# A decoder layer on one core: state products, rotation table and weight rounding in the front stage, last two token tiles in one round

## The reference

```
mod = silu(c) @ w_ada + b_ada                     # 6 vectors: sh1 sc1 g1 sh2 sc2 g2
u = modulate(rmsnorm(x), sh1, sc1) @ w_in          # 1024 columns
pool_out = pooling windows 2/4/8/16 of u[:, :512], minus u, then a 128x128 matrix per group
ssm_out  = state space mixer of u[:, 512:], 32 groups of 16 columns, 64 complex states each:
           h[t] = lambda * h[t-1] + B u[t];  y = Re(C h) + D u;  gelu(y) * sigmoid(gelu(y) @ glu_w + glu_b)
x = x + g1 * (concat(pool_out, ssm_out) @ w_out)
h2 = modulate(rmsnorm(x), sh2, sc2)
router: softmax over 4 groups, top 1; top 2 of its 4 experts; gated MLP experts (hidden 256)
x = x + g2 * moe(h2);  y = rmsnorm(x)
```

## Time and profile before

| what | us |
|---|---|
| median of 3 runs | 1243.48 (1240.98 to 1244.09) |
| profiled execution | 1243.06, its span 1241.1 |
| busy: PE, PEld, DVE, ACT, POOL | 1049.5, 798.2, 755.6, 514.4, 258.4 |
| 262 to 324, last block of the front: PE, DVE | 54.07, 9.60 of 62 |
| 324 to 336, PE and DVE | 0.00 and 0.17 of 12 |
| 392 to 469, scans and outputs y: PE, DVE | 70.92, 67.32 of 77 |
| 469 to 680, token tiles: PE, DVE | 201.16, 141.53 of 211 |
| 722 to 1150, experts: PE | 401.41 of 428 |
| DVE, front: first four w_lo parts; powers after them | 54.32 + 4.63; 58.86 to 64.42 |
| ACT, modulating one turned k-step (L667) | 0.778, median |
| DVE beside POOL, 128x256 two-input passes from 227.06 on | 227.06 + 0.41, then 227.39 + 1.28 and the next at 228.71 |
| POOL, busy stretches from 283 on | 282.86 to 284.35, 288.29 to 296.33, 302.08 to 303.35 |
| DVE, tile 15: residual ends, mean starts, h2 done | 692.92, 694.15, 697.31 |
| DVE, sample tile 16: the same | 701.20, 702.41, 705.55 |
| last logits | 710.21 + 0.17 |

### The profile page before, as it was taken

The page is one execution under the profiler, slowest core; times in us unless marked ns, Lnnn a source line. Parts: engine busy times, 40 slices in busy tenths (PEclk is TensorE's granted clock), DMA queues, the critical chain, the costliest instruction groups (busy, mean ns, idle before and its releaser), DMA issues. The chain is left out here.

```text
span 1241.1 us, 18046 instructions
## 1 busy us (share of the span) xinstructions
PE 1049.5 (85%) x5428; PEld 798.2 (64%) x5429; DVE 755.6 (61%) x1234; ACT 514.4 (41%) x764; POOL 258.4 (21%) x319
## 2 busy tenths in 40 slices
PE   5599999997568999997999535999999999999910
PEld 3266676674446767786888424887778878778710
DVE  2746475750289983367887686555676555555336
ACT  2522333221152235444665313455655544445325
POOL 0025252534131000000000001233333332232210
PEclk9699999998779999998999857999999999999955
DMA  9814646474592549466766457698789878765479
GB/s 304 324 35 115 205 114 201 118 228 162 147 198 90 167 140 265 157 175 233 239 209 224 134 201 250 163 293 217 218 263 267 223 212 222 220 154 110 88 206 394
DMA packets 173443, 244.74 MB, mean 197 GB/s; under 512 B 70519, under 2 KB 130631, under 8 KB 170263
## 3 DMA queue, kind: packets, MB, share of 16 engines
q1 hardware_dynamic: 148617, 180.31, 45.6%
q0 software_dynamic: 12528, 45.62, 16.1%
q10 hardware_dynamic: 12246, 18.14, 4.2%
HBM read 167.79 MB, written 75.84 MB: 196 GB/s over the span
## 5 line engine op out<-in xcount | busy, mean ns | idle before, releaser
L120 PE MATMUL experts_psGU<-weights_we_hi,experts_x_hi 128*128 (+1 forms) x344 | 144.9, 421 | 8.2 <-DVE experts_x_lo L2344 6.5
L121 PE MATMUL experts_psGU<-weights_we_hi,experts_x_lo 128*128 (+1 forms) x344 | 137.6, 400 | 0.0
L122 PE MATMUL experts_psGU<-weights_we_lo,experts_x_hi 128*128 (+1 forms) x344 | 137.5, 400 | 0.0
L120 PE MATMUL front_psM<-front_hT_hi,front_w_hi 128*128 128x512 f32 x256 | 105.7, 413 | 0.0
L2241 POOL DMA_INDIRECT acc_d<-experts_o_sb,experts_to_col x43 | 72.7, 1690 | 150.3 <-issue 67.0
L121 PE MATMUL front_psM<-front_hT_hi,front_w_lo 128*128 128x512 f32 x256 | 100.4, 392 | 0.0
L122 PE MATMUL front_psM<-front_hT_lo,front_w_hi 128*128 128x512 f32 x256 | 100.1, 391 | 0.0
L120 PEld LDWEIGHTS experts_psGU<-weights_we_hi,experts_x_hi 128*128 128x128 f32 x344 | 65.7, 191 | 34.1 <-issue 19.3
L2344 DVE TENSOR_TENSOR experts_x_lo<-experts_psX,experts_x_hi 128x1024 fp32r<-128x1024 f32 x44 | 53.9, 1225 | 40.1 <-ACT experts_x_hi L2277 40.1
L2334 DVE TENSOR_TENSOR weights_we_lo<-weights_we_raw,weights_we_hi (+1 forms) x64 | 75.5, 1220 | 4.1 <-ACT weights_we_hi L2268 3.1
L122 PEld LDWEIGHTS experts_psGU<-weights_we_lo,experts_x_hi 128*128 128x128 f32 x344 | 65.6, 191 | 15.7
(11 more groups left out here) (441 smaller groups left out, 2442.0 us busy)
## 6 DMA issues: line engine op xcount, KB each, us to landing
front_raw<-in_w_ada SPq DMA_DIRECT2D x32, 512.0 KB, 4.0
weights_we_raw<-in_exp_w_gate SPq DMA_DIRECT2D x16, 1024.0 KB
weights_we_raw<-in_exp_w_up SPq DMA_DIRECT2D x16, 1024.0 KB
weights_wd_raw<-in_exp_w_down SPq DMA_DIRECT2D x16, 1024.0 KB, 13.2
front_raw<-in_w_ada SPq DMA_DIRECT2D x8, 1024.0 KB, 10.9
front_xraw<-in_x_prompt SPq DMA_DIRECT2D x4, 2048.0 KB, 10.0
part_d<-middle_ev ACTq DMA_DIRECT2D x16, 512.0 KB, 3.1
middle_xt<-in_x_prompt SPq DMA_DIRECT2D x16, 512.0 KB, 4.5
```

The costliest lines, as they stand in the source:

```text
L120: pe.matmul(out, l_hi, r_hi, start=start, stop=False)
L121: pe.matmul(out, l_lo, r_hi, start=False, stop=False)
L122: return pe.matmul(out, l_hi, r_lo, start=False, stop=stop)
```

## The change

- **Start of the front.** SP loads half 0 of w_in, x and the sample rows ahead of the adaLN weights. ACT rounds w_hi of half 0 and DVE makes w_lo of half 0 and the powers before they normalise x. PE turns k-steps in the loop of product (0, 0), two ahead of the k-step that it multiplies, and waits for each tile's lo part. The sample products stand behind product (0, 0) and product (0, 1), where the first was ahead of both. PE's transposes for the tables stand before the adaLN matmuls.
- **End of the front.** DVE builds the rotation table (`rotations`) once product 28 of 32 is done, in passes of at most 256 numbers. PE computes the 32 state products behind the last kk_product, into the banks psT and psM, and DVE copies each of them, 264 columns, into H. SP loads the raw upper half of w_out into wp_raw after product 32, ACT rounds it to wp_hi. The last VB chunk is stored one product earlier. H, E, wp_raw and wp_hi get fixed addresses that both stages share.
- **Start of the middle.** `pool_half(0)` is first on PE. DVE makes two quarters of wp_lo, one token split, the other two quarters, one split, and then scans. POOL zeroes T behind wp_lo.
- **End of the middle.** The last gates are made one or two rounds earlier, and the residuals of the tiles 15 and 16 stand next to each other, with both norms behind.

```diff
-        w_lo = k.sb(st, "w_lo", [P, KD, D], F32R)
+        H_SIZE, E_SIZE = 2 * PAIRS * (NCH + 1) * 4, 2 * PAIRS * HC * 4
+        T.h_at = k.where["cT"]
+        k.skip_to(st, T.h_at + H_SIZE)
+        w_lo = k.sb(st, "w_lo", [P, 2, KD, BLK], F32R)
...
+        T.wp_at = k.where["hT_hi1"] + WP_SKIP
+        H = T.H = k.at("H", [P, 2, PAIRS, NCH + 1], T.h_at)
+        E = T.E = k.at("E", [P, 2, PAIRS, HC], T.e_at)
+        wp_raw = T.wp_raw = k.at("wp_raw", [P, QH, D], T.e_at + E_SIZE)
+        wp_hi = T.wp_hi = k.at("wp_hi", [P, QH, D], T.wp_at, F32R)
...
+                def w_load(h):
+                    sp.dma_start(wraw[h][:], w[:, :, h * BLK:(h + 1) * BLK]).then_inc(w_in[h], 16)
+
+                w_load(0)
+                sp.dma_start(xraw[:], a["x_prompt"][0, 0:BLK, :].rearrange("(j p) d -> p j d", p=P)
+                             ).then_inc(s["x_in"], 16)
+                sp.dma_start(x_smp[:], x_s).then_inc(s["xs_in"], 16)
                 for t in range(4):
                     ada_first(t)
...
                     gs = slice((m - QH) * GB, (m - QH + 1) * GB)
                     sp.wait_ge(ust_out[m % 2], 16 * STEP * (2 * (NBLK - 1) + (m - QH) // 2 + 1))
...
                     sp.dma_start(U[:, gs, NCH - CB:NCH], u_d[:, gs, NCH - CB:NCH]).then_inc(s["u_last"], 16)
+
+                def out_weights():
+                    sp.wait_ge(s["mm_done"], KD * NBLK)
+                    for i in range(2):
+                        c = slice(i * BLK, (i + 1) * BLK)
+                        sp.dma_start(wp_raw[:, :, c], a["w_out"][0].rearrange("(k p) n -> p k n", p=P)[:, 0:QH, c]
+                                     ).then_inc(wp_in, 16)

...
                             if b + 1 == NBLK:
                                 last_load(m)
...
+                            if b + 1 == NBLK:
+                                vb_store(NCK - 1)
                             kk_store(2 * b)
                         if m == 7:
                             if b + 2 < NBLK:
                                 x_load(b + 2)
-                            vb_store(2 * b + 1)
+                            if b + 1 < NBLK:
+                                vb_store(2 * b + 1)
                             cl_store(2 * b + 1)
...
                         pe.wait_ge(s["lo_done"], 8 * b + 8)
                     if b == 0 and m in (0, QH):
                         pe.wait_ge(s["w_l"], 4 * (m // QH) + 4)
                     if 8 * b + m >= 2:
                         pe.wait_ge(s["u_evac"], 8 * b + m - 1)
-                    elif m == 0:
-                        pe.wait_ge(s["hs_lo"], 1)
                     for t in range(KD):
-                        mm = matmul3(pe, psM[:, m % 2, :], w_hi[:, t, m * P:(m + 1) * P], w_lo[:, t, m * P:(m + 1) * P],
+                        if 8 * b + m == 0:
+                            if t + 2 < KD:
...
+                pe.wait_ge(s["ct_sb"], 1)
+                for t in range(NA - 1):
                     ada_first(t)
...
+                ada_first(NA - 1)
                 pe.wait_ge(s["mod_sb"], 1)
                 for q in range(4):
                     mm = pe.transpose(psC[:, q * P:(q + 1) * P], modA[:, q * P:(q + 1) * P], idt[:])
                 mm.then_inc(s["modt_ps"], 1)
-                for t in range(2, KD):
-                    turn(0, t, P, TPB)
-                pe.wait_ge(s["hs_lo"], 1)
-                pe.wait_ge(s["modt_sb"], 4)
-                pe.wait_ge(s["w_l"], 4)
-                sample_product(0)
                 for b in range(NBLK):
                     for m in range(KD):
                         product(b, m)
+                        if b == 0 and m == 0:
+                            pe.wait_ge(s["hs_lo"], 1)
+                            pe.wait_ge(s["modt_sb"], 4)
+                            sample_product(0)
...
+                for p in range(PAIRS):
+                    if p == 0:
+                        pe.wait_ge(s["vb_out"], 16)
+                        pe.wait_ge(s["hf_done"], KD * NBLK)
+                    if p % (GB // 2) == 0:
+                        pe.wait_ge(s["u_last"], 16 * (p // (GB // 2) + 2))
+                    if p == VB_KEEP * CP:
+                        pe.wait_ge(tst_out[1], 16 * NCK)
+                    for i in range(2):
+                        x = v_bank(pe, 2 * p + i)
+                        for g2 in range(2):
+                            mm = pe.matmul(x[NS * g2:NS * g2 + NS, :], VB[:, i, p, NS * g2:NS * g2 + NS],
+                                           U[:, 2 * p + g2, :], start=True, stop=True)
+                        mm.then_inc(s["x_fill"], 1)

             @block.scalar
             def _(act):
...
                 norm(0, P, TPB)
...
-                    act.wait_ge(w_in[h], 16)
-                    for j in range(4):
-                        act.copy(w_hi[:, 2 * j:2 * j + 2, h * BLK:(h + 1) * BLK], wraw[h][:, 2 * j:2 * j + 2, :]
-                                 ).then_inc(s["w_h"], 1)
-                act.wait_ge(s["s_mm"], 1)
-                act.copy(u_s[:, 0, :], psC[0:TS, :]).then_inc(s["us_done"], 1)
+                weights_hi(1)
...
+                act.wait_ge(wp_in, 32)
+                for i in range(4):
+                    c = slice(i * W4, (i + 1) * W4)
+                    act.copy(wp_hi[:, :, c], wp_raw[:, :, c]).then_inc(wp_h, 1)
...
+                def rotations():
+
+                    dve.wait_ge(s["mm_done"], KD * (NBLK - 1) + QH)
+                    dve.tensor_copy(E[:, 0, :, 0], ph[:, 2, 0, :])
+                    ch.link(dve.tensor_copy(E[:, 1, :, 0], ph[:, 2, 1, :]))
+                    for j in range(LOG_CH - 1):
+                        m = 2 ** j
+                        w = min(m, EW)
+                        t = [t4[:, i, 0:PAIRS * w].rearrange("p (k c) -> p k c", k=PAIRS) for i in range(4)]
+                        for c0 in range(0, m, EW):
+                            bc = [ph[:, 2 + j, i, :].unsqueeze(2).broadcast_to([P, PAIRS, w]) for i in range(2)]
+                            cmul(E[:, 0, :, m + c0:m + c0 + w], E[:, 1, :, m + c0:m + c0 + w], E[:, 0, :, c0:c0 + w],
+                                 E[:, 1, :, c0:c0 + w], bc[0], bc[1], t)
+
...
+                    for n in range(n0, n1):
+                        dve.wait_ge(s["x_fill"], FILLS + n + 1)
+                        dve.tensor_copy(H[:, n % 2, n // 2, 1:NCH + 1], (psT, psM)[n % 4 // 2][:, n % 2, 0:NCH]
+                                        ).then_inc(s["v_ev"], 1)

...
+                weights_lo(0)
...
+                more_powers()
...
-                weights_lo(0)
-                more_powers()
                 weights_lo(1)
                 input_rows()
...
+                    if b + 1 == NBLK:
+                        rotations()
...
+                state_inputs(0, 8)
                 kk_diag(NCK - 1)
...
+                state_inputs(8, 2 * PAIRS)
...
+                for i in range(2):
+                    ins = dve.tensor_copy(vs[:, i], H[:, i, :, 1:NSEQ + 1])
+                ch.link(ins)
+                for i in range(2):
+                    ins = dve.memset(H[:, i, :, NSEQ:NSEQ + 1], 0.0)
+                ch.link(ins)
...
+GATE_MID = {NT - 5: GLUS - 3, NT - 4: GLUS - 1}
+GATE_END = {t: t + LEAD for t in range(NT - 5)} | {NT - 5: GLUS - 2}
+
+
+def gates_of(t):
+    return [at[t] for at in (GATE_MID, GATE_END) if t in at]
...
+                for t in range(2):
+                    m_load(t)
...
-                for t in range(2):
-                    m_load(t)
                 for q in range(2):
                     cl_load(q)
+                for t in range(2, 4):
+                    m_load(t)
...
+                pool.wait_ge(s["wp_l"], 4)
                 pool.memset(T[:], 0.0).then_inc(s["t_zero"], 1)
...
+                        if t == 0:
+                            pe.wait_ge(s["wp_l"], 2 * c + 2)
...
+                pool_half(0)
                 pe.wait_ge(s["smp_in"], 112)
...
+                route(NBLK - 1, range(TPB - 1))
                 turn(LAST - 1)
-                route(NBLK - 1)
+                route(NBLK - 1, range(TPB - 1, TPB))
...
+                turned(LAST - 2)
+                for t in (LAST - 1, LAST):
+                    square(t)
+                    root(t)
+                turned(LAST - 1)
+                route_out(NBLK - 1)
...
+                out_lo(0)
+                out_lo(1)
...
-                    m_split(t)
+                m_split(0)
+                out_lo(2)
+                out_lo(3)
+                m_split(1)
...
+                residual(LAST - 1)
+                residual(LAST)
+                for t in (LAST - 1, LAST):
+                    mean(t)
+                    normed(t)
```

215 lines of the change are left out of this document (102 added, 113 removed).

## The result

| kernel | median, us | ratio to before, 95% interval |
|---|---|---|
| before | 1243.57 (1240.98 to 1244.09) | |
| changed | 1227.05 (1225.25 to 1230.23), 4 runs | 0.9875 (0.9857 to 0.9893) |

The account below looks back on a forecast made before the run. The front was taken as bound by PE and the middle as keeping PE and DVE busy, so only holes could be gained: 4.8+19.5+4.4 = 28.7 us off 1243.06 gives 1214.4 us; eight of ten cases in 1204 to 1226.

Parts of the forecast that it names:

- Part 1: Start of the front, to the first second-part (256-column) adaLN matmul: 72.86 us becomes 68.1, a gain of 4.8 us.
- the last adaLN block comes 4.8 us later: 43.0: Start of the front: the moved 2.10 MB load at 436 GB/s delays the last adaLN block from 38.20 to 43.0 us.
- a cold start: Rival, start of the front: PE stays at 1.2 GHz through the interleaved product; first part becomes -2, 1221 us; chance 0.15.
- Part 2: From the front's end to the middle's first output product: 392.45 us becomes 372.9, a gain of 19.5 us.
- 2.1 MB at 330 to 436 GB/s end at 333 to 334, the piece takes 3.0 us to land: 336: End of the front: U's last piece, queued behind two weight loads, lands at 336 us for the last eight state products.
- a late U: Rival, front's end and middle: U's last piece or T comes late; second part's gain becomes 12.7, 1220 us; chance 0.14.
- ACT's four roundings, about 4.2 us from 334, end before: End of the front: ACT's rounding of wp_hi, about 4.2 us from 334, ends before the middle starts at 341.4.
- T: Start of the middle: T's loads end at 369 to 376 us, 0 to 3 us late; taken as 0.
- The memset: Middle: POOL's zeroing beside DVE's scan costs 0 by the skill's rule; up to 3.5 us by a copy's row, giving 1217.
- Part 3: Last tiles, at the end of the middle: earlier gates 0.9 us, tiles 15 and 16 together 3.5; gain 4.4 us.
- +7.95 ... +17.7. Gain 3.5: Last tiles: from residual 15, both residuals done at +7.95, last logits at +17.7 instead of 21.2 us; gain 3.5.
- slower rival (rotation table): Rival, end of the front: DVE's rotation table outgrows its 31.5 us cover and delays the state products; 1248 us; chance 0.03.

Follow-up runs that it names:

- rounds_old: The changed kernel with tiles 15 and 16 each in its own round and one whole route, as before; 1225.74 us, ratio 0.9861 to the kernel before.
- gates_old: The changed kernel with the last gates where they were, one round after the other; 1231.59 us, ratio 0.9906 to the kernel before.
- same_again: The changed kernel run and profiled again without an edit; 1227.19 us, ratio 0.9876 to the kernel before.
- start_only: The kernel before with only the change's start of the front, w_lo in two halves and no gap ahead of it; 1237.04 us, ratio 0.995.
- shift_before: The kernel before with 128 bytes skipped ahead of w_lo, so it and all behind it in the front lie higher; 1250.09 us, ratio 1.0053.
- aligned: The changed kernel with its large front buffers 896 bytes higher, w_lo at 55808, the 128-byte gap kept; 1224.23 us, ratio 0.9844 to the kernel before.
- ev_zero: The changed kernel with acc_d zeroed early from a small buffer, so T's loads need not wait for it; 1227.91 us, ratio 0.9883 to before.
- u_first: The changed kernel with U's last piece loaded ahead of the two w_out loads; 1226.21 us, ratio 0.988 to the kernel before.
- wlo_layout: The kernel before with w_lo laid out in two halves of 512 columns at the same address; 1242.72 us, ratio 0.9993.
- all512: The changed kernel with w_hi at 22528 and w_lo at 55296, 32768 bytes apart, at multiples of 512; 1224.94 us, ratio 0.9834 to the kernel before.
- shift_all: The kernel before with 128 bytes skipped ahead of w_hi, so w_hi, w_lo and all behind move together; 1246.22 us, ratio 1.0016.
- best_all: best_u with the buffer placement of all512 instead of that of aligned; 1219.78 us, ratio 0.9809 to the kernel before.
- best_u: The changed kernel with aligned, rounds_old and u_first, and each half of wp_raw rounded as it lands; 1219.72 us, ratio 0.9807 to the kernel before.

## Why the prediction was right and wrong

The sum, by stretches of the profiles (mean of six with the old end of the front, of seven with the changed one and the gap ahead of w_lo; in the first row only the three of the six that have the old start and no shift; in the last without rounds_old and gates_old):

| part | forecast | measured | rests on |
|---|---|---|---|
| 1, to the last kk_product | 4.8 | 324.6-323.0 = 1.6 | 6.2 alone |
| 2, last kk_product to last output product | 19.5 | 141.5-125.3 = 16.2 | 17.0 in `same_again`, 12.2 in the slowest profile; 70.0-55.0 = 15 to the first output product |
| last output product to residual 0 | 0 | 73.4-73.4 = 0 | |
| 3, residual 0 to residual 15 | 0.9 | 152.8-152.3 = 0.5 | round 14: 9.4 to 8.2 |
| 3, residual 15 to last logits | 3.5 | 21.7-22.4 = -0.7 | 20.9 in rounds_old, 25.1 in gates_old |
| sum | 28.7 | 17.6 | 16.5 by the medians |

**Part 1: the mechanism was right, and the step that failed is "the last adaLN block comes 4.8 us later: 43.0".** Alone the edit is worth 6.2 us. In the change the block came at 47.55, and the last but one shows how: 35.77 before, 4.8 for the load (40.60 in start_only), 2.4 for w_lo's new address, together 43.0; then 4.5 us to the last one, where before it stood 2.43 behind. The address is the 128 bytes of `k.skip_to(st, T.h_at + H_SIZE)`: the diff shows that line, and I had read it as a matter of space. It costs 2.4 us at this mark also when nothing else is changed (38.10 in shift_before), and 6 ns in each product. The 4.5 us are 16 transposes that the change puts between the last two blocks, which the order rows show and I left out. They cost little at full clock (2.65 us in aligned) and 2 us more at the low level, which the profiles show now and then without an edit to this stretch (4.54 in the change, 2.65 in ev_zero); why PE has one level or the other there is open. Two further terms were off and partly cancel. The interleaved product was counted at 1.2 GHz for 6 us; it has clock 1.00 from 52 on, so from the first product (52.74) to the sample product (63.68) are 10.9 us where 13.8 were forecast. The sample product then took 7.2 instead of 5.5, half of it at 0.53. The rival "a cold start" was wrong in its place and right in that low stretches come, one before the product and one behind it. Of what is gained to the first 256-column adaLN matmul, the front's products take back 2 to 3 us on their way to the last kk_product (from the one to the other 252.9 us, mean of ten profiles of the new start at 395 ns; 250.4, mean of three at 389); the times of the runs don't resolve them.

**Part 2: the step that failed is "2.1 MB at 330 to 436 GB/s end at 333 to 334, the piece takes 3.0 us to land: 336".** The two loads were issued at 327.70, where I had them near 327.6, and were there at 337.25, 9.5 us later: 2.1 MB at 220 GB/s, with the u stores and the table stores in the same queue (304 GB/s from 328 to 338 in all). U's piece landed at 338.1, 9.0 us behind its issue; the 336 of the sum are 7. PE had been ready at 334.8 and stood for 3.33 us, and the eight products behind took 6.7 (5.5 in `same_again`) instead of 3.7, at clock 0.56: an end of the range that I had priced but not joined to its cause. It is the wait that brings the low level: with the wait gone (u_first) they run at full clock. The middle starts 23.1 us (21.6 in `same_again`) behind the last kk_product; 18.2 were forecast. The rival "a late U" is what happened, at 3.4 to 5 us. It missed that U isn't alone: "ACT's four roundings, about 4.2 us from 334, end before" still holds in the change, but by a start at 337.25 (and 3.88 us), and u_first shows that they hold the stage once U is early, which is why moving U alone gives only 1 us. The inner terms hold: state products at 0.44 us, the table's end at 310.76 (311), its cover 3.72 (3.5), scans 7.1 us into the middle (7.4).

**T:** I took 0 and kept 3 as an end. T's last load landed 0.9 us behind H in the one profile and ahead of it in `same_again`; what came late, by 3.65 and 2.3 us, was the first output product, which waited for an eviction of ACT behind a token tile that SP loads after T. No term of the sum has that wait. ev_zero, which moves T and that tile up together, takes it away and gains nothing: the scans follow one another on DVE. So 0 was right for the time, for another reason than air on PE.

**The memset:** the two-input passes at 353.56 to 355.37 took 0.68 and 0.69 us beside POOL's memset of 3.52, no more than the 0.69 to 0.72 of the earlier trace rows without it, and the small COPY at 356.09 took 0.57, ending with the memset at 356.6. The Trainium skill (SBUF — State Buffer, "Who interferes with whom") says that a DVE instruction with two SBUF inputs contends with a GpSimd one that reads SBUF, not with one that only writes it. The trace agrees for these passes: the 3.5 us that the row of a copy would have given did not come. That a copy is held up by a memset is seen again: the same copy takes 0.17 us at 380.50, without one.

**Part 3: the step that failed is the round of two tiles, "+7.95 ... +17.7. Gain 3.5".** It counted the DVE tiles nearly right (norm of 16 done at 692.26, 15.2 behind residual 15; 14.3 forecast) and got two things wrong. Residual 16 waited 1.67 us for the load of its `part`, which I had not counted, and began 5.4 us behind residual 15 instead of 4.2. And behind the norm I counted 3.4 us for turn, h2T, route of 16 rows and logits: it took 6.9, since PE was still at the route of tile 15, which takes 3.49 us for the one tile where four take 3.30 (rounds_old), at the low level after PE had stood for 6.52 us. The gates were put too low, at 0.9, because I priced them in the old order of rounds; with the new one they are worth 3 us by the trace and 3.7 by the times.

**The rest.** That the change is faster was given 0.96 and holds. Of the rivals, the cold start and late U each described a part of the truth, and both came at once; the range was worked out as if one at a time would. The late U's 12.7 for part 2 gives 1221.2 and not 1220, and the row of the memset 1217.9 and not 1217; neither slip matters. The slower rival (rotation table) was rightly small.

## What to carry to other kernels

Look in a diff for every address that moves, also by 128 bytes: here another placement gave 4 to 5 us back, nearly the 6.2 that a whole part of the change gained, and nothing in the order of instructions shows it. Read a mark at the instruction that waits for the load, not at one behind it: the last adaLN matmuls met the forecast to 0.1 in a run where two terms were off. Price a load by what a queue gives at that place with everything else in it, not by the best rate of the trace, and where it makes PE wait, ask for the low clock behind the wait. When one wait is taken away, write down what the second holder of the same barrier is, and price an edit in the new order of the work, not in the old one.

## What the runs showed of the hardware

- Loads of short rows into buffers moved up by 128 bytes: 193 GB/s (179 in wlo_layout, at the same addresses) became 105 (shift_before); 93 in the changed kernel, and 183 and 178 with w_lo back at a multiple of 512 (aligned, all512). With w_hi moved as well it was 149 (shift_all), with w_lo at the address of the 105, so the multiple of 512 is not all of it. Nor is 512 as such shown: w_lo's fast places (54784, 55296, 55808) are multiples of 256 too, its slow one (54912) of 128 only.
- fp32r matmuls of 128x512: median 389 ns with w_hi and w_lo 32768 bytes apart (before, start_only, shift_all, all512, best_all), 395 with 32896 (shift_before, the change, aligned, best_u); the hT tiles lie 128 bytes farther from w_hi in the second group as well. Within a product the matmuls lie 0.227 and 0.233 us apart.
- A route of one tile (16 matmuls into one group of 32 columns) took 3.49 us at granted clock 0.53 (692.4 to 695.9 us), one of four tiles (64 into four groups) 3.30 in rounds_old and 3.27 in before, both at 0.58: by these times four column groups run side by side.
- After 3.3 us of standing PE worked at 0.56 for the 6.7 us that followed; after 1.9 us a stretch at 0.53 came too (64 to 67.5 us). Matmuls and transposes taking turns, 5.53 us busy of 6, kept clock 1.00 (52 to 58 us).
